# Last two expert blocks kept in PSUM and scattered to the outputs, with smaller moves at the start of the expert stage

## The reference, cut to what matters

```python
a = jax.nn.silu(xb @ w1[e]) * (xb @ w3[e])
return ((a @ w2[e]).astype(jnp.float32) * w[:, None]).astype(h.dtype)
...
x = x + hier_moe(h2, w_grp, w_exp, w1, w3, w2).reshape(B, L, D_MODEL)
...
y_prompt = rmsnorm(yp, g_final)
y_sample = rmsnorm(ys, g_final)
```

## Time and profile before

| what | us |
|---|---|
| median of 3 runs | 1022.72 (1022.17 to 1023.6) |
| the profiled execution, its own time | 1020.73 |
| its span in the trace | 1019.0 |
| TensorE busy | 965.6 |
| VectorE busy | 740.3 |
| ScalarE busy | 443.9 |
| GpSimd busy | 219.4 |

### The profile page before, as it was taken

How to read it: one execution, slowest core, us unless ns; L and a number is a source line. 1 busy time by engine, 2 the same in 40 slices (tenths; PEclk the granted TensorE clock), 3 DMA queues, 4 the chain that set the end, 5 groups by cost and what they waited for, 6 DMA issues and landing times.

```text
span 1019.0 us, 16208 instructions
## 1 busy us (share of the span) xinstructions
PE 965.6 (95%) x5356; PEld 835.9 (82%) x5357; DVE 740.3 (73%) x1631; ACT 443.9 (44%) x739; POOL 219.4 (22%) x225
## 2 busy tenths in 40 slices
PE   6999999999999999999999999969999999999970
PEld 6998898988889888898886888857888888888860
DVE  5965466855678556685558666589999999999965
ACT  6621122121221212212113112148988998898864
POOL 0001220012200122001221100031443443443220
PEclk9999999999999999999999999979999999999995
DMA  9511105111051110512027332389999999999938
GB/s 317 179 42 54 42 22 176 40 53 39 25 173 41 54 34 29 173 33 80 35 81 261 150 140 103 117 310 408 394 393 393 391 401 388 392 395 382 340 50 333
DMA packets 74627, 190.21 MB, mean 187 GB/s; under 512 B 12519, under 2 KB 47443, under 8 KB 62131
## 3 DMA queue, kind: packets, MB, share of 16 engines
q1 hardware_dynamic: 61099, 159.07, 41.1%
q0 software_dynamic: 13312, 29.69, 9.9%
q10 hardware_dynamic: 144, 0.52, 0.2%
HBM read 167.43 MB, written 38.68 MB: 202 GB/s over the span
## 4 chain that ended last, share of the span: by engine, by line
PE 86%; DVE 6%; DMA 4%; ACT 1%; issue 1%; SPq 0%; POOL 0%; DVEq 0%; POOLq 0%; ACTq 0%
PE bank L2007 17%; PE bank L887 12%; PE bank L889 12%; PE bank L888 11%; PE bank L2008 9%; PE bank L918 8%; PE bank L1058 3%; PE bank L1996 1%; PE bank L958 1%; PE bank L2022 1%; PE bank L2030 1%; PE bank L2018 1%; PE bank L2026 1%; DVE x L1470 1%; DMA raw<-in_w_in_dram 1%
## 5 line engine op out<-in xcount | busy, mean ns | idle before, releaser
L1348 DVE TENSOR_TENSOR w_lo<-w,w_hi 128x1024 fp32r<-128x1024 f32 x128 | 150.3, 1216 | 0.1
L776 ACT ACTIVATE w_hi<-w 128x1024 fp32r<-128x1024 f32 x128 | 129.7, 1068 | 3.0 <-PE bank L889 2.9
L2007 PE MATMUL bank<-wvg_hi,hT_hi 128*128 128x512 f32 x256 | 104.4, 408 | 0.0
L887 PE MATMUL bank<-w_hi,xT_hi 128*128 128x512 f32 x256 | 102.9, 402 | 1.3 <-issue 1.3
L2007 PE MATMUL bank<-wvg_lo,hT_hi 128*128 128x512 f32 x256 | 100.9, 394 | 0.0
L2007 PE MATMUL bank<-wvg_hi,hT_lo 128*128 128x512 f32 x256 | 100.7, 393 | 0.0
L889 PE MATMUL bank<-w_hi,xT_lo 128*128 128x512 f32 x256 | 100.2, 391 | 0.0
L1814 ACT ACTIVATE v<-bank 128x256 f32<-128x256 f32 x32 | 12.3, 383 | 201.3 <-PE bank L2008 201.3
L888 PE MATMUL bank<-w_lo,xT_hi 128*128 128x512 f32 x256 | 99.7, 389 | 0.0
L2362 POOL TENSOR_TENSOR mixed<-onorm,pgate 128x256 f32<-128x256 f32 x36 | 38.9, 1080 | 272.4 <-DVE onorm L2178 272.4
L887 PE MATMUL bank<-hT_hi,wuqk_hi 128*128 128x344 f32 x288 | 94.1, 327 | 0.1
(11 more groups left out here) (279 smaller groups left out, 2390.3 us busy)
## 6 DMA issues: line engine op xcount, KB each, us to landing
w<-in_w_dram SPq DMA_DIRECT2D x96, 1024.0 KB
raw<-in_w_in_dram SPq DMA_DIRECT2D x57, 256.0 KB, 3.2
mixed_d<-mixed POOLq DMA_DIRECT2D x32, 128.0 KB, 2.1
sample_state<-in_state_ret_dram SPq DMA_DIRECT2D x16, 256.0 KB, 3.7
out_dram<-sample_state SPq DMA_DIRECT2D x16, 256.0 KB, 3.6
mixed_in<-mixed_d SPq DMA_DIRECT2D x8, 512.0 KB, 4.2
x_again<-in_x_prompt_dram SPq DMA_DIRECT2D x8, 512.0 KB, 3.4
h_d<-h POOLq DMA_DIRECT2D x8, 512.0 KB, 3.0
```

Source lines behind the costliest of these rows:

```text
L776: act.activation(hi, whole_w, ACT.Copy).then_inc(S["up_hi"], 1)
L887: pe.matmul(out, lhs[0], rhs[0], start=first, stop=False)
L1348: dve.tensor_tensor(lo, whole_w, hi, ALU.subtract).then_inc(S["up_lo"], 1)
L2007: g = pe.matmul(gates, x[xi], wvg[wi][:, 1:3, k, :], start=first, stop=last)
```

## The change

- **The last two blocks (30 and 31, `HELD = 2`) are not scattered to `sum_d`.** Their pair weight is put on in the gate, and their down products stay in four PSUM banks. When the scatter of block 29 has landed, GpSimd gathers the rows of `sum_d` for the two blocks, and TensorE adds them in the banks by a product with the identity (`z_mm`). Squares and scaling read the banks. The rows go to `y_prompt` by `idx_tok` and to `y_sample` by `sample_store`, each by an indirect DMA.
- **The end has 11 units** instead of nine tiles, in groups of 2, 3, 3 and 3. The samples' tile and tiles 0 to 2 are stored by SyncE as before. Tiles 3 to 7 are stored by GpSimd through `row_store`, which leaves out the held rows. A held unit waits until SyncE's four stores have landed. The tiles are loaded into `fin`, which lies over free weight slots. SyncE starts when both `sum_out` have reached 15 scatters each.
- **Tables for that** (`store_rows`) are made by VectorE at the end of steps 24 to 28: in step 24 the spill count, in step 25 its register load, in 26 to 28 eight small instructions.
- **The register load of the spill count** is in step 24 on ScalarE and in step 25 on VectorE. On the other engines it stays behind the stage.
- **The bounds of GpSimd's indirect DMAs** come from registers that are set once. An indirect gather that moves no row stands before the third tile's copies in the stage before.
- **`pair_weights`** on VectorE stands ahead of `x_low(0, 0)`.
- ScalarE's table load for the square root moves from behind the stage into step 31.

```diff
-            x_low(0, 0)
             pair_weights()
+            x_low(0, 0)
             weight_planes()
...
                 for q in range(DOWNS):
                     down_high(b, s % SLOTS, uses(s, g), q)
-
+                if isinstance(b, int) and b == NE - ROUND:
+                    many_act.append(spill_count(act))
...
                     down_low(b, s % SLOTS, q)
+                if isinstance(b, int):
+                    store_rows(b - (NE - ROUND))
...
+                if step == 0:
+                    spill_total()
+                elif step == 1:
+                    many_dve.append(spill_count(dve))
...
-            for b in range(NE - SLOTS, NE):
+            for b in range(NE - SLOTS, NE - HELD):
                 scatter(b, b - ROUND * ROUNDS, ROUNDS, icol[b % ROUND][:, :])
...
+            for b in range(NE - 1, NE - 1 - HELD, -1):
+                pool.wait_ge(xg_in[b % SLOTS], 16 * MAIN_USES[b % SLOTS])
+                pool.indirect_dma_start(out=xg[b % SLOTS][:, :], out_offset=None, in_=sum_d,
+                                        in_offset=indexed(idx_tok[:, b:b + 1]),
...
+                if kind == "tile":
+                    pool.indirect_dma_start(out=y_prompt[0], out_offset=indexed(row_store[:, t:t + 1]),
...
+                pool.wait_ge(y_out, 16 * PLAIN)
```

More of the change, by code:

```diff
@@ L343, in step_kernel @@
         junk_f = rc.place("junk_f", [P, D], F32)
+        no_row = rc.place("no_row", [P, 1], I32)
+        ov_wide = rc.place("ov_wide", [P, NE, 8], F32)
+        over = rc.place("over", [P, 1], F32)
+        held = rc.place("held", [P, 2 * NT], F32)
+        held_rows = rc.place("held_rows", [P, CH], F32)
+        row_pair = rc.place("row_pair", [P, CH], I32)
+        row_store = rc.place("row_store", [P, CH], I32)
+        far = rc.place("far", [P, HELD], F32)
+        sample_store = rc.place("sample_store", [P, HELD], I32)
+        assert rc.at <= whole.end
+        fin = nc.alloc_sbuf_tensor_at("fin", [P, NT, D], F32, offset=at_W)
+        assert at_W + NT * D * 4 <= rm.where["w2_1"]
+        y_spill = nc.alloc_sbuf_tensor_at("y_spill", [P, D], F32, offset=ry.where["w2_hi_end"])
         SS, MS, RS = 0, 9, 18
@@ new lines, in more, with root_of_units @@
+                y_out_of_psum(b, y_spill)
+            spilled(act, many_act[0], more, save_held, sqrt_again)
+            def root_of_units(a, b):
+                for n in range(a, b):
+                    if UNITS[n][0] == "held":
+                        act.wait_ge(S["mean_done"], after(NE - UNITS[n][1]))
+                return act.activation(small[:, MSF + a:MSF + b], small[:, SSF + a:SSF + b], ACT.Sqrt,
+                                      bias=small[:, EPSC:EPSC + 1])
+            squares = 0
@@ new lines, in stage_c_act @@
+            for n, (kind, t) in enumerate(UNITS):
+                if kind == "tile":
+                    r, at = rows_of(t), ORDER.index(t)
+                    act.wait_ge(rows_in[at], 48 if at == CH else 32)
+                    act.wait_ge(S["sq_done"], after(SQ3 + squares))
+                    act.activation(junk_f[r, :], fin[r, t, :], ACT.Square, scale=D ** -0.5,
+                                   accum_out=small[r, SSF + n:SSF + n + 1]).then_inc(S["sq_done"], 1)
+                    squares += 1
+                else:
+                    for q in range(2):
+                        act.wait_ge(S["z_mm"], after(2 * (NE - 1 - t) + q + 1))
+                        act.wait_ge(S["sq_done"], after(SQ3 + squares))
+                        act.activation(junk_f[:, 0:512], down_bank(t, q), ACT.Square, scale=D ** -0.5,
+                                       accum_out=small[:, SSZ + 2 * (NE - 1 - t) + q:SSZ + 2 * (NE - 1 - t) + q + 1])\
+                            .then_inc(S["sq_done"], 1)
+                        squares += 1
@@ L1477, in stage_c_dve @@
                     a, b = NORM_GROUPS[n]
-                    dve.wait_ge(S["root3_done"], after(n + 1))
-                    do(rsqrt_columns(steps, dve, *(small[:, at + a:at + b] for at in (SS, MS, HX, RS, TX))))
+                    for m in range(a, b):
+                        if UNITS[m][0] == "held":
+                            mean_of_halves(m)
+                    dve.wait_ge(S["root_done"], after(ROOT3 + n + 1))
+                    do(rsqrt_columns(steps, dve, *(small[:, at + a:at + b] for at in (SSF, MSF, HXF, RSF, TXF))))
                 else:
```

281 lines of the change are left out of this document (195 added, 86 removed).

## The result

| | before | after |
|---|---|---|
| median of 4 runs each | 1022.44 us | 1033.09 us |
| lowest and highest | 1019.74 and 1023.6 | 1031.4 and 1034.87 |
| ratio, 95% interval | | 1.0105 [1.0082, 1.0128] |
| profiled execution: time, span | 1020.73, 1019.0 | 1034.77, 1033.1 |

The change makes the kernel slower by 10.65 us. I had predicted 1.3 us, and a range that ended at 1028.5. So both the number and the range were wrong.

The account below looks back on a forecast made before the run. TensorE bounds the expert stage, DMA is 93% busy at the end. Start -1.0, wait 2.8 and additions 0.9 end the stage 2.75 us later; with the end, the span grows 1.3, so 1024.0 us, range 1018.5 to 1028.5.

Parts of the forecast that it names:

- The end: After block 31: GpSimd's queue of stores decides; end at 1017.5 us, or 1020.25 with the stage's 2.75 us.
- With 0.3 to the end: Last step of the sum: 0.3 us from the landing of tile 7's store to the program's end, giving 1017.5.
- the forecast's choice: GpSimd's plain indirect stores at the end priced like gathers: four at 1.48 and three at 1.29 us, 9.8 together.
- the first rival: At the end, plain stores cost what adding scatters cost: 13.0 instead of 9.8 us, 3.7 more in all, 1027.7; chance 0.2.
- The wait in step 24: ScalarE's register load waits for VectorE's spill count, delaying block 26's high parts; TensorE loses 2.8 us.
- the load's: ScalarE's register load in step 24: 0.49 and 0.17 us and a short check, 0.7 us together.
- a rival with a chance of 0.1 and 2.5 us: In the expert stage, the wait's idle time lowers TensorE's clock; half a clock over some 5 us costs 2.5: 1026.5.
- dense work on both sides: Argument against the clock falling at the wait in step 24: the hole is short, with dense work around it.
- VectorE's additions in steps 25 to 28: VectorE's register load and small instructions in the stage add 0.9 us, bounds 0 and 2.4.
- The start: Start of the expert stage: pair weights moved into VectorE's idle time, and the empty gather; -1.0 us, bounds 0.8 and 1.3.
- what is cold: Start of the stage: the empty gather may take the first gather's extra cost (2.10 against 0.99 us), 1.1 us at most.

## Why the prediction was wrong

**The end: the step that failed is its last one, "With 0.3 to the end".** I ended the sum where the last bytes land. 7.0 us of drain were missing, three quarters of the whole error of 9.35 us (10.65 measured, 1.3 predicted). The row was there in the trace of before: GpSimd's sequencer busy from 993.9 to 1002.2 behind its last instruction. I looked at who was last to work, but not at what each engine still does once it has nothing to do, because on SyncE, which was last then, it is 7 ns. The change moved the end of the program to another engine, and its closing cost came with it. None of my rivals had this.

Without the drain the end was right in sum: from block 31's turn to the landing of the last store I had 1020.25 - 0.3 - 974.6 = 45.4, and it took 1025.7 - 980.15 = 45.6. That close it is in part by luck, as three misses cancel. Block 31's first store starts 1.4 later than I had worked out (0.8 of it behind the tiles' scaling, 0.6 between the scaled halves and the store), from there to tile 7's store it is 9.3 instead of 9.8, and that store lands 3.5 behind its start instead of 4.2. The 0.6 is a wait that I had listed among the changes and left out of the sum: a held unit's store waits until SyncE's four have landed. That plain stores cost what gathers cost (0.98 and 0.30, not 1.55) was the forecast's choice, and the first rival fell. This is also the side on which the Trainium skill stands, in Collectives: The Full Stack, section on the bandwidth ceiling: a copy has one read descriptor where an add has two.

**The wait in step 24: right in mechanism and place, too small in size.** Predicted was 2.8 with the count in it. Without the clock it cost 0.9 for the count and 2.34 for the load, 3.24 together, so 0.4 over the sum: TensorE's idle time in after is 2.65. The term that was too small is the load's: from the end of the count (927.75) to ScalarE's next instruction (928.92) it is 1.17 us, where I had 0.7, for the register load's three rows have gaps between and behind them. The fall of the clock (1.4) I had as a rival with a chance of 0.1 and 2.5 us; it happened in both profiles of after, behind holes of 2.65 and 2.69 us, so 0.1 was too low. My reason against it, dense work on both sides, didn't hold. The Trainium skill (TensorE: Matmul & The Clock Gate, "What's actually happening") says that the clock follows how busy the array has been lately; the trace agrees with it here, as the clock falls behind the hole and stays full where the hole is 0.31.

**VectorE's additions in steps 25 to 28: right.** Predicted 0.9; the intervals behind the turns of blocks 28 and 30 are 0.7 and 0.4 too long in after, and moving them out gave 0.95.

**The start: right in size, half right in cause.** 0.8 in the first profile of after and 1.24 in the second, 1.0 predicted. The 0.8 to 0.9 put on the pair weights is there in every profile that has them at full clock, among other edits; alone at full clock they weren't profiled. The empty gather does not take "what is cold" out of the first one: a build is slow when it starts within one of VectorE's instructions, and the 2.10 us of the first gather in before were such a one.

**Together:** -0.8 for the start, -1.2 for the end without the drain, +7.0 drain, +3.2 wait, +1.4 clock and +1.1 additions are 10.7 by the traces, beside 10.65 by the medians. The closeness says little: from block 31's turn to the end, two profiles with the same code there, both of after, differ by 0.5 us, and the one of before and the two with the pair weights first by up to 1.9 (46.9 to 48.9).

## What to carry to other kernels

When a change lets another engine finish last, look up what that engine does after its last instruction, in a trace in which it finishes early; here a mere wait on GpSimd at the end costs 5.5 to 6 us. Let GpSimd's program end as early as it can, and let another engine wait for its DMAs. A wait put into a full pipeline is priced by the slack of the engine behind it, and then by the clock; and a number that many engines need, as the spill count here, should be made early, but loaded on each engine only as early as that engine needs it.

## What the runs showed of the hardware

- GpSimd's drain at the end of the program takes 6.9 to 8.4 us, whether its last DMA was 25 us ago or is still in flight. ScalarE's takes 0.33, SyncE's 0.007, VectorE's 1.45 in kernels with the end of before and 3.73 in those with that of after. GpSimd's is 6.9 to 7.0 in all kernels with an empty indirect gather and 8.3 to 8.4 in all without. The cause stays open.
- TensorE's clock fell to 1.2 GHz behind a hole of 2.65 us in a stage of full load, for some 3 us. A hole of 0.31 us at the same place didn't do it.
- Building an indirect gather takes 0.99 us. If it starts within one of VectorE's 1.14 us instructions for the low parts of weights, what is left of that instruction comes on top: 401 of 402 such gathers fit within 0.08 us, and they take from 1.06 to 2.15.
- An indirect store that doesn't add mostly takes 0.98 us to build (1.36 at most), with 0.30 to the next; one that adds mostly takes 1.55 to 1.60.
